# A chunked recurrence rewritten as products without its state, its outputs' mean taken out beforehand, and four element-wise steps moved to GpSimd

## What is computed

```python
def rwkv7_scan(r, decay, k, v, kk, a):
    def step(S, inp):
        r_t, w_t, k_t, v_t, kk_t, a_t = inp
        sa = jnp.einsum('bhvk,bhk->bhv', S, -kk_t)
        S = (S * w_t[:, :, None, :]
             + sa[..., None] * (kk_t * a_t)[:, :, None, :]
             + v_t[..., None] * k_t[:, :, None, :])
        y = jnp.einsum('bhvk,bhk->bhv', S, r_t)
        return S, y
    ...

def rwkv7_group(p, mu, w0, w_up, a0, a_up, k_k, k_a, r_k, ln_w, ln_b):
    ...
    pf = pf + mu * (prev - pf)
    r, k, v, gate, wd, ad = split_cols(pf, RWKV_SIZES)
    ...
    y = rwkv7_scan(r, decay, k, v, kk, a)
    mean = jnp.mean(y, axis=-1, keepdims=True)
    var = jnp.mean(jnp.square(y - mean), axis=-1, keepdims=True)
    y = (y - mean) * lax.rsqrt(var + RWKV_GN_EPS) * ln_w.reshape(H, N) + ln_b.reshape(H, N)
    y = y + jnp.sum(r * k * r_k, axis=-1, keepdims=True) * v
    y = y.reshape(B, T, RWKV_WIDTH) * jax.nn.silu(gate)
    return y.astype(p.dtype)
```

## Time and profile before

| | us |
|---|---|
| median of 3 runs | 2165.74 |
| lowest, highest | 2164.93, 2173.73 |
| the profiled execution | 2172.61 |
| its span in the profile | 2171.4 |
| PE busy in it | 2030.9 (94%) |
| DVE, ACT, POOL busy | 1088.7, 873.4, 27.3 |
| first matmul of `w_out` (the mixers' end) | at 490.94 |

### The profile page before, as it was taken

How to read it: one execution, slowest core, us unless ns; L and a number is a source line. 1 busy time by engine, 2 the same in 40 slices (tenths; PEclk the granted TensorE clock), 3 DMA queues, 4 the chain that set the end, 5 groups by cost and what they waited for, 6 DMA issues and landing times.

```text
span 2171.4 us, 28244 instructions
## 1 busy us (share of the span) xinstructions
PE 2030.9 (94%) x11400; PEld 1613.2 (74%) x11400; DVE 1088.7 (50%) x1929; ACT 873.4 (40%) x1567; POOL 27.3 (1%) x68
## 2 busy tenths in 40 slices
PE   6898888889989999999999999999899999999997
PEld 5765666777766679878888887667478978888886
DVE  5666468737465454354334354444355445343444
ACT  5325443244345444343223243566644344232332
POOL 0000000000000000000000000011000000000000
PEclk9989899999999999999999999999999999999999
DMA  5210011012211123122222222111023212222221
GB/s 200 88 49 21 20 59 49 3 60 101 88 49 49 39 97 127 68 88 97 90 104 89 98 95 88 59 49 49 30 97 113 102 59 97 97 97 97 97 97 69
DMA packets 52050, 169.63 MB, mean 78 GB/s; under 512 B 5776, under 2 KB 9424, under 8 KB 51920
## 3 DMA queue, kind: packets, MB, share of 16 engines
q1 hardware_dynamic: 51920, 167.82, 22.1%
HBM read 165.70 MB, written 2.10 MB: 77 GB/s over the span
## 4 chain that ended last, share of the span: by engine, by line
PE 85%; DVE 9%; ACT 4%; issue 1%; DMA 0%; POOL 0%; SPq 0%; DVEq 0%; ACTq 0%
PE ps L152 83%; PE ps L157 3%; DVE ps L380 1%; DVE wr L171 1%; DVE X L1530 0%; DVE lo L218 0%; DMA cst<-d_cst 0%; DVE macc L233 0%; DVE ra_S L769 0%; DVE rc_S L769 0%; DVE rb_S L769 0%; DVE ra_Z L789 0%; ACT sa_sp L2103 0%; DVE x_acc L233 0%; ACT wr L165 0%
## 5 line engine op out<-in xcount | busy, mean ns | idle before, releaser
L152 PE MATMUL ps<-hi,wr 128*128 128x512 f32 (+1 forms) x4616 | 1406.9, 385 | 50.1 <-DVE wr L171 34.2
L152 PEld LDWEIGHTS ps<-hi,wr 128*128 128x128 f32 x4616 | 861.9, 190 | 230.2 <-DVE wr L171 25.7
L152 PE MATMUL ps<-lo,wr 128*128 128x512 f32 (+1 forms) x2308 | 879.9, 381 | 0.0
L152 PEld LDWEIGHTS ps<-lo,wr 128*128 128x128 f32 x2308 | 439.6, 190 | 84.1 <-issue 3.9
L165 ACT ACTIVATE wr<-raw 128x1024 fp32r<-128x1024 f32 x293 | 307.6, 1052 | 349.6 <-PE ps L152 349.6
L171 DVE TENSOR_TENSOR wr<-raw,wr 128x1024 fp32r<-128x1024 f32 x293 | 356.7, 1217 | 4.3 <-ACT wr L165 2.3
L1457 DVE TENSOR_TENSOR X<-X,ps 128x512 f32<-128x512 f32 x96 | 66.0, 688 | 238.3 <-PE ps L152 238.3
L1986 ACT ACTIVATE mlp<-mlp 128x512 f32<-128x512 f32 x64 | 40.4, 632 | 207.8 <-DVE mlp L1969 207.8
L1969 DVE SCALAR_TENSOR_TENSOR mlp<-ps,R 128x512 f32<-128x512 f32 x64 | 44.3, 692 | 113.2 <-PE ps L152 106.2
L213 ACT ACTIVATE hi<-X,pv 128x512 fp32r<-128x512 f32 x48 | 34.7, 722 | 138.2 <-DVE X L1457 136.2
L1972 DVE TENSOR_TENSOR lo<-mlp,hi 128x512 fp32r<-128x512 f32 x64 | 44.3, 693 | 87.8 <-ACT hi L1990 87.8
(11 more groups left out here) (696 smaller groups left out, 1877.4 us busy)
## 6 DMA issues: line engine op xcount, KB each, us to landing
raw<-d_w SPq DMA_DIRECT2D x128, 512.0 KB, 3.4
raw<-d_wkv SPq DMA_DIRECT2D x32, 512.0 KB, 3.5
raw<-d_w_in SPq DMA_DIRECT2D x30, 512.0 KB, 3.5
raw<-d_sb_w_in SPq DMA_DIRECT2D x24, 512.0 KB, 3.4
raw<-d_ev_w_in SPq DMA_DIRECT2D x16, 512.0 KB, 3.4
raw<-d_wq SPq DMA_DIRECT2D x16, 512.0 KB, 3.5
raw<-d_wo SPq DMA_DIRECT2D x16, 512.0 KB, 3.4
X<-d_xT SPq DMA_DIRECT2D x16, 256.0 KB, 5.1
```

The lines of the kernel that those rows point to most:

```text
L152: return pe.matmul(out, lhsT, rhs, start=start, stop=stop, skip_group_check=True)
```

## The change

It concerns the pairs only. The following is what it does.

- The chunks' parts that don't hold the state are made for all four chunks at once. `kx` is transposed (four transposes, one bank) and copied by ACT to the tiles KB; u without the state (eight products S4 times vt, in round 1 of the inverse) is copied beside it. Two groups of four 128x128 products with XF then give A and B for all chunks (`ab`; ACT copies one bank, DVE the other).
- The state's recurrence becomes M(c) = gamma * (kt.vt + bt.B + P.M(c-1)), with P = 1 + A.bt made once (`pt`) and 64x64 states in the place of 128x128 ones. Outputs are v.S4 + B.S4 + M.(r + G), with G = S4.A added to `kr` by DVE (`g`). They come in two halves of two chunks.
- v is transposed by a product with the matrix 1 - ones/64 per head (`center`), so the outputs have no mean; the mean's product and subtraction are gone. ACT squares straight from the bank.
- `kh`, `bh`, `kx`, `rx` are six GpSimd instructions per pair. The first products wait for the last of them; so does ACT before it copies vt, kt, bt.
- The gate's mix moves from the pg step to round 1 of the inverse, its SiLU from the S4 steps to rounds 2 (ACT) and 3 (DVE), the clearing of XF to the end of round 5.
- A pair has 28 steps in the place of 36, so against the other lane everything behind pair 0's chunks comes earlier. `masks_vector` moves one step ahead.

```diff
@@ inverse_tensor
+    b = K.take(*k, "kx")
+    pe.wait_ge(*K.clear(*k, "kx"))
+    for c in range(4):
+        done = tr(pe, M, b[:, c * 128:c * 128 + 128], L.KR(c, 0))
...
+        if l == 1:
+            b = K.take(*k, "u")
...
+                    done = mm(pe, b[:, at:at + 64], L.S4[c][h][:, 0:128], L.vt[:, at:at + 64], at == 0, True)
@@ inverse_vector
+        if l == 1:
+            mixed_vector(K, M, v, (*k, "pg"), 12 + i, L.g, L.r)
+        if l == 3:
+            silu_vector(K, v, (*k, "pg", "mix"), L.r, L.g, L.g)
@@ rwkv_tensor
+            if name == "vt":
+                done = mm(pe, r3(b[:, cs], 2), src[:, cs], sh.center, c == 0, True)
...
-        b = K.take(*k, "xu", c)
...
-        b = K.take(*k, "y", c)
...
-    b = K.take(*k, "mean")
...
+    for z in range(2):
+        b = K.take(*k, "ab", z)
...
+            done = mm(pe, b[:, j * 128:j * 128 + 128], L.XF[:, at:at + 128], L.KB[z][:, j * 128:j * 128 + 128],
+                      j == 0, True)
+    yield
...
+    state_tensor(K, pe, k, L, 0)
...
+            done = mm(pe, b[half(h), c * 64 - 64:c * 64], L.A(c, h), L.bt[:, c * 128 + h * 64:c * 128 + h * 64 + 64],
+                      c == 1, True)
...
+            done = mm(pe, b[half(h), c * 128 - 128:c * 128], L.A(c, h), L.S4[c][h][:, 384:512], c == 1, True)
+    yield
...
+    state_tensor(K, pe, k, L, 1)
+    outputs_tensor(K, pe, k, L, 0)
+    yield
+    state_tensor(K, pe, k, L, 2)
+    yield
+    outputs_tensor(K, pe, k, L, 1)
     yield
+def state_tensor(K, pe, k, L, c):
...
+        mm(pe, b[half(h), 0:64], L.kt[:, at], L.vt[:, at], True, False)
+        done = mm(pe, b[half(h), 0:64], L.bt[:, at], L.B(c, h), False, not c)
+    if c:
+        for h in range(2):
+            done = mm(pe, b[half(h), 0:64], L.PT[half(h), c * 64 - 64:c * 64], L.M[half(h), c * 64 - 64:c * 64],
+                      False, True)
+def outputs_tensor(K, pe, k, L, z):
...
+            mm(pe, out[h], L.vt[:, c * 128 + h * 64:c * 128 + h * 64 + 64], L.S4[c][h][:, 128:256], c % 2 == 0, False)
+            done = mm(pe, out[h], L.B(c, h), L.S4[c][h][:, 384:512], False, not c)
+                done = mm(pe, out[h], L.M[half(h), c * 64 - 64:c * 64], L.KR(c, 1)[half(h), :], False, True)
@@ rwkv_vector
-    v.tensor_tensor(L.k, L.k, L.sg, ALU.mult).then_inc(*K.tell("dve", *k, "kh"))
-    v.tensor_tensor(L.a, L.a, L.sg, ALU.mult).then_inc(*K.tell("dve", *k, "bh"))
...
-    v.scalar_tensor_tensor(out=y, in0=K.bank(*k, "mean"), scalar=-1.0 / 64, in1=y, op0=ALU.mult,
-                           op1=ALU.add).then_inc(*K.tell("dve", *k, "yc", frees=(*k, "mean")))
+def state_vector(K, v, k, L, c):
...
+    v.tensor_scalar(L.M[:, c * 64:c * 64 + 64], K.bank(*k, "m", c)[:, 0:64], L.st[:, 4 + c:5 + c], None,
+                    ALU.mult).then_inc(*K.tell("dve", *k, "M", c, frees=(*k, "m", c)))
@@ rwkv_pool
+    g.wait_ge(*K.done("act", *k, "E"))
+    g.wait_ge(*K.done("dve", *k, "rk"))
+    g.tensor_tensor(L.k, L.k, L.sg, ALU.mult).then_inc(*K.tell("pool", *k, "kh"))
+    g.tensor_tensor(L.a, L.a, L.sg, ALU.mult).then_inc(*K.tell("pool", *k, "bh"))
+    for z, base in enumerate((L.kr0, L.kr1)):
...
```

More of the change, by code:

```diff
@@ L663, in masks_vector @@
         v.tensor_copy(M.first.eye[half(q), :], M.C("ident")[half(q), half(q)]).then_inc(*K.tell("dve", "eye"))
+    v.scalar_tensor_tensor(out=M.first.center, in0=r3(M.C("blk"), 2), scalar=-1.0 / 64, in1=r3(M.C("ident"), 2),
+                           op0=ALU.mult, op1=ALU.add).then_inc(*K.tell("dve", "center"))
 QUARTERS = [(c, h, q) for c in range(4) for h in range(2) for q in range(2)]
@@ L721, in inverse_tensor @@
         done.then_inc(*K.tell("pe", *k, "t", l))
+        if l == 1:
+            b = K.take(*k, "u")
+            pe.wait_ge(*K.clear(*k, "u"))
+            pe.wait_ge(*K.done("act", *k, "vt"))
+            for c in range(4):
+                for h in range(2):
+                    at = c * 128 + h * 64
+                    done = mm(pe, b[:, at:at + 64], L.S4[c][h][:, 0:128], L.vt[:, at:at + 64], at == 0, True)
+            done.then_inc(*K.tell("pe", *k, "u"))
         if l < 5:
@@ L813, in inverse_scalar @@
 def inverse_scalar(K, M, a, k, L):
[L814 removed]
     yield
     yield
+    columns_scalar(K, a, k, L, "kx")
     yield
@@ L836, in inverse_scalar, with columns_scalar @@
     yield
+def columns_scalar(K, a, k, L, name):
+    a.wait_ge(*K.done("pe", *k, name))
+    for z in range(2):
+        to = L.KB[z].rearrange("p (j w q) -> p j w q", j=4, w=2)[:, :, 0 if name == "kx" else 1, :]
+        a.activation(to, r3(K.bank(*k, name)[:, z * 256:z * 256 + 256], 4), ACT.Copy).then_inc(
+            *K.tell("act", *k, name, frees=(*k, name)))
 def rwkv_tensor(K, M, pe, i, L):
@@ L917, in rwkv_tensor @@
-    b = K.take(*k, "mean")
-    pe.wait_ge(*K.clear(*k, "mean"))
-    pe.wait_ge(*K.done("act", *k, "y", 3))
-    mm(pe, b, M.C("blk"), M.Y[i], True, True).then_inc(*K.tell("pe", *k, "mean"))
+    pe.wait_ge(*K.done("act", *k, "u"))
+    pe.wait_ge(*K.done("dve", *k, "XF"))
+    for z in range(2):
+        b = K.take(*k, "ab", z)
+        pe.wait_ge(*K.clear(*k, "ab", z))
+        for j in range(4):
+            at = z * 512 + j * 128
+            done = mm(pe, b[:, j * 128:j * 128 + 128], L.XF[:, at:at + 128], L.KB[z][:, j * 128:j * 128 + 128],
+                      j == 0, True)
+        done.then_inc(*K.tell("pe", *k, "ab", z))
@@ new lines, in rwkv_tensor @@
+    yield
+    pe.wait_ge(*K.done("act", *k, "bt"))
+    pe.wait_ge(*K.done("act", *k, "ab", 0))
+    state_tensor(K, pe, k, L, 0)
+    pe.wait_ge(*K.done("dve", *k, "ab", 1))
+    b = K.take(*k, "pt")
+    pe.wait_ge(*K.clear(*k, "pt"))
+    for c in (1, 2):
+        for h in range(2):
+            done = mm(pe, b[half(h), c * 64 - 64:c * 64], L.A(c, h), L.bt[:, c * 128 + h * 64:c * 128 + h * 64 + 64],
+                      c == 1, True)
+    done.then_inc(*K.tell("pe", *k, "pt"))
+    b = K.take(*k, "g")
@@ L1021, in rwkv_vector @@
-    y = M.Y[i]
-    v.wait_ge(*K.done("pe", *k, "mean"))
-    v.scalar_tensor_tensor(out=y, in0=K.bank(*k, "mean"), scalar=-1.0 / 64, in1=y, op0=ALU.mult,
-                           op1=ALU.add).then_inc(*K.tell("dve", *k, "yc", frees=(*k, "mean")))
+    yield from inverse_vector(K, M, v, k, L, i)
+    v.wait_ge(*K.done("pe", *k, "ab", 1))
+    v.tensor_copy(L.AB[1], K.bank(*k, "ab", 1)).then_inc(*K.tell("dve", *k, "ab", 1, frees=(*k, "ab", 1)))
+    yield
+    state_vector(K, v, k, L, 0)
+    v.wait_ge(*K.done("pe", *k, "pt"))
@@ L2222, in pool_program @@
 def pool_program(K, M, g):
+    for i in range(4):
+        rwkv_pool(K, g, i, M.rwkv[i])
     sb_layer(M, lambda z, L: sb_pool(K, g, z, L))
```

192 lines of the change are left out of this document (93 added, 99 removed).

## The result

| | us |
|---|---|
| kernel before, 20 runs | 2168.07 (2164.20 to 2173.73) |
| changed kernel, 20 runs | 2175.87 (2169.11 to 2181.40) |
| ratio | 1.003, 95% interval 1.0022 to 1.0039 |
| profiled execution | 2170.89, span 2169.7 |
| first matmul of `w_out` in it | at 492.38 |

The change costs 0.3%. They are good for what waits for what. For the time the runs have to be taken.

The account below looks back on a forecast made before the run. PE was taken as the bound, busy 94%, with 53.0 us idle before `w_out`. Products +6, waits -17.6, clock -7 and GpSimd +3 gave -15.6, so 2157.0 for the profiled execution and 2150 as median; range 2138 to 2163.

Parts of the forecast that it names:

- The wait among the `nsa` heads, 217 to 323: PE's idle time there: pair 1's dense products, S4 and rounds fill pauses, 8 of 14.1 us left, -6.
- The clock: Windows with long waits have a lower granted clock; shrinking waits return up to half of 13.3 us, -7.
- The prediction's own sign of being wrong: In 217 to 392, the granted clock staying at 0.92 would show the prediction wrong.
- The products: PE's recurrence work: 10.9 us per pair go, 12.4 come, 1.5 more per pair, +6 us in all.
- The `wr` waits of pairs 2 and 3: PE's two waits from 323 on, 6.0 and 4.0 us, shrink as less DVE work stands ahead, -5.
- S4 and rounds of pairs 2 and 3: From 392 on: S4 and first-round waits vanish, later rounds' waits rise to 5 of 8.2 us, -3.3.
- Rival 2: Mix and SiLU inside the inverse's rounds expose them, 9 to 10 us back: -5.6, 2160; chance 0.15.
- The tail: Idle time in 474 to 491: mean and subtraction go, Ln, Exp and DVE steps stay, 5.8 left, -2.3.
- GpSimd: forecast +3: kh, bh, kx, rx on GpSimd are covered, but contention with DVE costs between 0 and 9.4 us, taken as +3.
- Rival 3: GpSimd holds DVE up at the single price where DVE is last, 9.4 us: -9.2, 2156.5; chance 0.14.
- The slower rival: GpSimd costs double and holds DVE 9.4 us ahead of a `wr` in all four pairs: +19, 2185; chance 0.06.
- pair 0's preparation (forecast -1): Before 217, kh, bh and kr are off DVE for pair 0, so PE waits less: -1.

Follow-up runs that it names:

- e1: Changed kernel with eight empty steps between pair 0 and pair 1, putting pair 1 back in its old place: 2168.30 us, ratio 0.9997 to before.
- e3: Changed kernel with eight empty steps between pairs 0 and 1 and kh, bh, kx, rx back on DVE: 2169.30 us, ratio 0.9991 to before.
- e11: e3 with the eight empty steps spread, one or two behind each of pair 0's seven last steps: 2163.79 us, ratio 0.9974 to before.
- e2: Changed kernel with kh, bh, kx and rx back on DVE at their old places: 2175.49 us, ratio 1.0026 to before.
- e7: e3 with the gate's mix, SiLU and clearing back at their old places, leaving products and centering: 2172.16 us, ratio 1.0013 to before.
- e8: e1 with one weight unit made ahead of the decay scans of pairs 2 and 3 on DVE: 2167.73 us, ratio 0.9985 to before.
- e4: Kernel before with only kh, bh, kx and rx moved to GpSimd: 2171.07 us, ratio 1.0007 to before.
- e5: Kernel before with only the gate's part (mix, SiLU and clearing of XF moved into the inverse's rounds): 2164.30 us, ratio 0.9970 to before.
- e6: Kernel before with only the centered values, without mean product and subtraction: 2169.16 us, ratio 0.9998 to before.
- e9: Kernel before with the gate's move and the centered values, without the new products: 2165.28 us, ratio 0.9978 to before.

## Why the prediction was wrong

**The wait among the `nsa` heads, 217 to 323: forecast 14.1 to 8, measured 14.1 to 25.1. This step failed.** (In the fixed window 230 to 330 it is 14.0 to 20.7.) The order was read rightly (pair 1's dense products, S4 and rounds between the heads), and then only PE's side of it was counted, as filler. A dense step comes with eight DVE steps, and DVE's queue is in order, so they stand ahead of the softmax that PE waits for. What the prediction said of `wr`, that whatever stands ahead of it can hold it up, holds for L401 as well: PE's waits for it went from 1.9 to 17.7 us. e1 and e3 show it: 6.4 and 7.4 us at full clock come back, and all but 3.7 and 3.2 of the waits for L401 go, when only pair 1 is moved back, and with it what follows it in the lane. e11 shows the rest: the chunk products of pair 0, which filled pauses of the heads before, had to be dealt out as well, for another 2.4 us at full clock (error 1.0).

**The clock: forecast -7, measured +6.4 in the ledger, some 4 us of it in time. This step failed too.** The prediction's own sign of being wrong came true: the granted clock is 0.93 from 217 to 323 and 0.88 from 323 to 392, where it was 0.92 and 0.93. Even with 6.5 and 8.4 us less idle time up to `w_out` than before the change, as in e3 and e11, the share rises by 5 to 6; it does so in every kernel with the new products as made (e1, e2, e3, e7, e8, e11: +4.3 to +6.6) and in none without (e4, e5, e6, e9: -3.9 to +1.9). So the rule "fewer pauses, more clock" was not this kernel's. In part the new work was put where the clock is low anyway: u of pair 0 at 3.67 instead of 2.00. From 130 to 230 the granted clock is 0.90 on average in the seven kernels with the products and u early, 0.93 in the two with u late and 0.92 in the five without the products. The rest, 2 to 3 us of the share, stays open. The traces point to 230 to 330 without settling it: the granted clock is 0.88 to 0.93 there in nine kernels with the products and 0.91 to 0.97 in five without (0.91 and 0.94 on average), one trace each, and in the traces of before and of the change it is the same, 0.91. What in the products lowers it wasn't tried, so the cause of this part isn't shown.

**The products: forecast +6, measured about -1.** The mechanism was right, the prices were too high, and with them the term's sign turned. Idle and clock's share taken off, PE's time to `w_out` is 376.9 us before and 375.8 after (from windows of 5 us). The rows that stand for the terms, in the changed kernel's PE timeline:

```profile
471.29 1.95 PE L152 MATMUL ps<-rc_KB,rc_XF 128*128 128x128 f32 x16
473.17 0.34 PE L152 MATMUL ps<-rb_vt,rb_kt 128*64 128x64 f32 x4
...
474.34 0.34 PE L152 MATMUL ps<-rc_vt,rc_kt 128*64 128x64 f32 x4
...
475.46 0.34 PE L152 MATMUL ps<-rb_vt,rb_kt 128*64 128x64 f32 x4
...
482.74 0.44 PE L152 MATMUL ps<-rc_S,rc_vt 128*64 128x128 f32 x4
...
484.65 1.12 PE L152 MATMUL ps<-rb_tmp,cst 128*128 128x512 f32 x2
```

Eight products with XF take 1.88 (471.29 to 473.17), 0.235 each and not 0.33. The first state, P and G, 8 + 6 products with their 64-column forms, take 1.12 (474.34 to 475.46) where 0.155 and 0.13 apiece gave 2.0. The last outputs, eight products and four with M, take 1.91 (482.74 to 484.65), where 0.155 and 0.11 apiece gave 1.7. The centering costs 0.89 for four products (404.25 to 405.14; the centering matrix lies in a tile of `lm`) against 0.44 for four transposes (405.14 to 405.58), so 0.45 and not 0.85:

```profile
404.25 1.05 PE L152 MATMUL ps<-lm,rc_v 128*128 128x128 f32 x8
405.14 0.60 PE L157 MATMUL ps<-cst,rc_k 128*128 128x128 f32 x4
405.58 0.60 PE L157 MATMUL ps<-cst,rc_a 128*128 128x128 f32 x4
```

The 0.33 was the start-to-start distance of a single product between two different groups; in a long group of equal ones they come closer. The dear prices made the forecast more cautious, by 7 us, so it is not why it missed.

**The `wr` waits of pairs 2 and 3: forecast 5, measured 6.4** (3.3 and 3.1, where the signs were 3 and 2; 10.0 before). Near. **S4 and rounds of pairs 2 and 3: forecast 4.9, measured 5.7** in 409 to 480. Near as well, and no wait for an S4 tile of 0.4 us or more is among them. e5 shows what had been ahead of S4: with the gate's part alone its waits fall from 2.4 to 0.5 us and the time at full clock by 2.4. Rival 2, the exposed rounds, is refuted by the same run, and by e7 and e3 in the new arrangement, where the gate inside the rounds takes 4.6 us off at full clock.

**The tail: forecast 5.8 idle, measured 5.75**, behind the same chain as in the earlier trace rows:

```profile
492.38 0.77 PE L152 MATMUL ps<-hi,wr 128*128 128x512 f32 x1 [5.75 <-ACT hi L1511]
```

**GpSimd: forecast +3 against DVE without these steps.** The price per 128x512 was 1.26 alone and up to 2.27 beside DVE, inside 1.18 to 2.35. No wait of PE is put down to GpSimd in the changed kernel's trace, so the cover held. DVE is held up, which no row of before had shown (6.8 us of stretch, partly off the path). What the move costs in all, contention less relief, is 0.5 to 1.7 us at full clock with errors of 0.7 to 1.1: +0.7 from e2 to the change, +1.7 from e3 to e1, +0.5 in e4. The Trainium skill's rule for two SBUF inputs (SBUF — State Buffer, "Who interferes with whom") is borne out on both sides: DVE's row at 76.73 takes 2.05 in the place of 1.22, and GpSimd's row at 387.24 takes 2.27 in the place of 1.26 beside DVE's `wr`. L401 and L621 have one SBUF input and are stretched too. The page says that such an instruction contends when it runs in a two-port mode; no run here shows in which mode they ran. Rival 3 saw the mechanism but not that DVE's relief balances it, within these errors.

**The slower rival** had its sign from GpSimd. The sign came from two places which had no rival of their own: DVE's queue among the `nsa` heads, and a clock that takes instead of gives. The median, 2175.87, lies just inside the prediction's band for no change (2154.9 to 2176.6), though the runs do tell it from no change.

The sum: at full clock -8.6 was forecast, -17.6 of it for idle time. In the two traces idle time up to `w_out` rises by 0.8: +11.0 among the heads, -3.2 for the stretch of the `wr` waits (344 to 409), -2.5 for S4 and the rounds, -2.4 in the tail, -0.4 in pair 0's preparation (forecast -1) and -1.8 ahead of 130, where none was forecast. With -1 for the products that gives -0.2, where +0.6 was measured over all runs (GpSimd's part, where it costs anything, is in the idle time). The clock's share turned from -7 to +6.4. Together +7.0 in the place of -15.6.

## What to carry to other kernels

When a woven stage gets shorter, list what now stands beside what on every engine, and price the partner's instructions on the in-order engine that the other lane waits for; empty steps are a cheap way to test and to undo it. Don't book the clock as a gain from fewer pauses: split each run into time at full clock and the clock's share, and book the first alone. Test the parts of a combined change by themselves: here the two small ones (the gate's place, the centering) held 6.2 us of gain at full clock. The large one added 3.7 to that, of which the ledger's bias may be 1.2, once its steps were dealt out among the other lane's (e11), and the clock took it back: in time e11 (0.9974) can't be told from the two small parts alone (0.9978).

## What the runs showed of the hardware

- A two-input float32 GpSimd instruction of 128x512 takes 1.26 us and one of 128x256 0.73 us when DVE leaves it alone, up to 2.27 and 1.72 when not (changed kernel, 74 to 82, 283 to 290 and 375 to 394 us). DVE instructions beside it take up to 1.9 us longer for a pair (2.78 for 0.88), also those with one SBUF input.
- Runs of one kernel differ by 5 to 15 us in this case, and the granted clock goes with it: in the 35 runs of before beside e1 to e4 the span and the clock's share have a correlation of 0.96. A run whose clock's share is 1 us higher is only 0.63 us longer (254 runs).
- Float32 products 128 deep of 128x128 in a long equal group come every 0.235 us, and those recorded as 128*128 with 128x64 every 0.23 (eight from 332.83 to 334.67): halving the columns on that side saved nothing. Where the other side is halved (128*64), six products of 128x128 take 0.65, 0.11 each (changed kernel's PE timeline; the next row starts at 475.46):

```profile
474.81 0.88 PE L152 MATMUL ps<-rc_S,rc_AB 128*64 128x128 f32 x12
```
